# Grid attention of a two-model kernel: values held stationary, gates computed turned, the spatial norm on ScalarE and GpSimd

## The chip, the cores and the metric

The kernel runs on one core of one Trainium2 chip. The metric is the time of one execution in device microseconds, as the median of several runs. The core has five engines that run their own instruction streams in order and wait for one another by semaphores: TensorE (matrix products, PE in the profile, with weight loads as PEld), VectorE (DVE), ScalarE (ACT), GpSimd (POOL) and SyncE (SP), which here issues the large DMA transfers. TensorE writes to eight banks of PSUM of 128x512 fp32 values; a bank can be written again when an engine has read it and said so.

## The reference

Two blocks are computed one after the other, in fp32. The first has two layers of a mixture of retention, sparse attention and gated linear attention. The second has two layers on 256 tokens and 256 context tokens, D = 1024. The change lies in the second block's first layer, for 512 rows in all (4 tiles of 128; tiles 0 and 1 are tokens, 2 and 3 context):

```python
q, k, v, u, vv, gate = split(hl @ w_in)        # q 512, k 128, v 128, u 512, vv 512, gate 1024
a = windowed_sink_gqa(q, k, v, kc, vc, sink)   # 8 heads of 64, 2 key/value heads, softmax with a sink
b = chunk_gmlp(gelu(u), gelu(vv), ln_g, ln_b, w_s, b_s)
y = (concatenate([a, b], axis=-1) * silu(gate)) @ w_out
yc = (concatenate([ac, bc], axis=-1) * silu(gate_c)) @ w_out   # the same for the context rows

def chunk_gmlp(u, v, ln_g, ln_b, w_s, b_s):    # per chunk of 128 rows and group of 64 columns
    vn = layer_norm(v, ln_g, ln_b).reshape(B, n, 128, 8, 64)
    s = einsum('gpq,bnqgc->bnpgc', w_s, vn) + b_s
    return u * s
```

The softmax of one head divides by the sum of exp(logit - max) over the keys plus exp(sink - max). Token rows see 512 keys, context rows 256. In the second block's other layer (the odd layer) the attention is of another kind; it is not changed.

## The kernel before, in words

Products of high precision are made of three: each operand is split into a part rounded to fp32r ("high") and the rest ("low"), and TensorE adds high by high, high by low and low by high. Weight chunks come by DMA into a ring of three slots (`ring`); ScalarE copies a piece to the high part (`wide_high`), VectorE subtracts to get the low part (`wide_low`). For weights of the grid layer a chunk is four pieces of 128x1024, and the four chunks are e_g0 and e_g1 (the gate's two halves) and e_o0 and e_o1 (the output projection). The rows are `xhi` and `xlo`, turned so that the contraction lies on the partitions. `project_wide` (L1138) makes 24 products of 128x512 for one tile of rows.

The attention of the grid layer is a hand-written pipeline of `E_STEPS` = 15 steps, written once for each engine. There are 24 units (`E_UNITS`): a token tile with one head, or a context tile with two heads, so a unit always has 512 logits per row. In step g, TensorE does in this order:

1. a gate projection if `E_GATES` has one (e_g0 for tiles 0 to 3 in steps 0 to 3, e_g1 in steps 7 to 10);
2. row sums of a modulation chunk (`E_SUMS`, L734), their columns (`E_ADA`, L742), gate rows (`E_ROWS_AT`, L1157);
3. the turning of the probabilities of pair g-2 (`e_turn`, units 2g-4 and 2g-3, L771);
4. the logits of pair g (`e_logits_pair`, L1235, 64 contraction rows, the two units side by side in the row halves);
5. the value products of pair g-3 (`e_values`, L1219), with turned probabilities stationary and values moving, into bank `eo{t}` as rows by heads;
6. in step 4 the spatial products of `w_s` with the normed `evv` (`gs0` to `gs3`, L1290); in steps 12 and 13 the turning of gated rows (`turn_mixed`, eight blocks of 128x128 for a tile); in step 14 the first output projection.

ScalarE applies tanh to a gate (L1803), copies turned probabilities out of the bank (L1449), takes the exponentials with their row sums (L1819, L1824), and once for a tile the sink's exponential (L1836). VectorE finishes the gate's silu (`e_silu`, L2618), scales and masks the logits (L2650), reduces the maximum (L2653), takes the minimum with the negated sink (L2655), adds the sink (L2663), does two operations of the spatial norm in each of steps 0 to 3 (L2590, L2592), adds and multiplies the spatial results (L2679), and makes the low pieces (L2559). The division by the softmax's sum comes last, in `e_gated` (L2601 to L2610), on the 128x512 result of a tile, followed by the product with the gate. `e_mixed` (L2626) makes the spatial half of the gated rows. ScalarE and VectorE then split the turned rows into `xhi` and `xlo` (L1755, L2634).

Banks 0 and 1 are given in turn to projections, sums, columns, gate rows and spatial products (`proj()`); banks 4 and 5 hold the logits of a pair, 6 and 7 turned probabilities, 2 and 3 the attention results. The order in which the banks' users appear in `units_of_layer_e` is the order in which they must be freed. GpSimd rotates queries and keys before the stage and is idle in it. Chunks are loaded in the order of the list `CHE`, each when the last user of its slot is done.

## Time and profile before

| | us |
|---|---|
| median of 3 runs (1067.85 to 1070.85) | 1068.13 |
| the profiled execution, its own time | 1068.55 |
| its span, first to last instruction | 1066.2 |
| TensorE busy | 1034.2 (97%) |
| VectorE busy | 611.4 (57%) |
| ScalarE busy | 487.0 (46%) |
| GpSimd busy | 76.4 (7%) |
| mean granted TensorE clock | 0.995 |

A busy share is an average over the whole span. Products are pipelined: the duration shown for one product overlaps the next, so the price of a block of products is the distance between its start and the start of what follows it. A product of two fp32 operands is recorded as two instructions, so sixteen instructions are eight products.

### The profile page before, as it was taken

What the parts mean: (1) busy time and instruction counts of PE and PEld (TensorE: products, weight loads), DVE (VectorE), ACT (ScalarE), POOL (GpSimd) and SP (SyncE); (2) the same over time, 40 slices, a digit from 0 to 9 for tenths busy, and PEclk for the clock granted to TensorE, in tenths of its full rate; (3) what the DMA queues carried; (4) which work ended last, traced back from release to release, by engine and by line L of the source; (5) the groups of instructions that cost most, each with busy time, mean ns of one, the idle gap of its engine ahead of it and who ended that gap; (6) DMA issues with size and microseconds to landing.
All of it is one profiled execution on the core that took longest, in us unless ns stands there. A gap on an engine that the chain in (4) does not pass through costs nothing.

```text
span 1066.2 us, 13509 instructions
## 1 busy us (share of the span) xinstructions
PE 1034.2 (97%) x5180; PEld 759.1 (71%) x5180; DVE 611.4 (57%) x1193; ACT 487.0 (46%) x958; POOL 76.4 (7%) x103
## 2 busy tenths in 40 slices
PE   7999999999999999999999999999999999999997
PEld 5788875777466887767875587777767888646565
DVE  2539866595656299754454653234754546135873
ACT  2536546562135365475540453246444433334872
POOL 3001110000000020110000000500000001212000
PEclk9999999999999999999999999999999999999999
DMA  9854442476625355235567353422443014433000
GB/s 384 314 200 166 158 158 81 158 312 270 251 88 197 135 195 202 106 115 216 218 237 310 124 199 121 158 99 80 182 178 137 4 40 157 179 111 146 2 1 39
DMA packets 13742, 171.27 MB, mean 161 GB/s; under 512 B 1504, under 2 KB 1760, under 8 KB 3056
## 3 DMA queue, kind: packets, MB, share of 16 engines
q1 hardware_dynamic: 13216, 168.82, 41.4%
q10 hardware_dynamic: 464, 1.61, 0.4%
q8 instruction: 41, 0.67, 0.3%
q14 instruction: 21, 0.17, 0.0%
HBM read 169.37 MB, written 1.05 MB: 160 GB/s over the span
## 4 chain that ended last, share of the span: by engine, by line
PE 83%; ACT 7%; DVE 6%; DMA 2%; issue 1%; SPq 0%; DVEq 0%; ACTq 0%
PE bank L800 15%; PE bank L1138 8%; PE bank L1087 8%; PE bank L1027 7%; PE bank L1185 6%; PE bank L771 5%; PE bank L1120 4%; PE bank L778 3%; PE bank L1322 3%; PE bank L872 3%; PE bank L1417 2%; PE bank L1144 2%; PE bank L1402 2%; PE bank L734 2%; DMA X<-in_x 1%; PE bank L1387 1%
## 5 line engine op out<-in xcount | busy, mean ns | idle before, releaser
L1526 ACT ACTIVATE whi<-ring 128x512 fp32r<-128x512 f32 x120 | 73.8, 629 | 67.8 <-PE bank L800 67.6
L800 PE MATMUL bank<-whi,xhi 128*128 128x512 f32 (+1 forms) x256 | 99.4, 388 | 1.3 <-ACT dsag L1449 1.3
L2208 DVE TENSOR_TENSOR wlo<-ring,whi 128x512 fp32r<-128x512 f32 x120 | 82.3, 707 | 29.8 <-ACT whi L1526 29.6
L800 PE MATMUL bank<-whi,xlo 128*128 128x512 f32 (+1 forms) x256 | 98.0, 383 | 0.0
L800 PE MATMUL bank<-wlo,xhi 128*128 128x512 f32 (+1 forms) x256 | 97.5, 381 | 0.0
L778 PE MATMUL bank<-ring,hT 128*128 128x512 f32 (+1 forms) x160 | 61.8, 540 | 1.8 <-ACT hT L1469 1.8
L1027 PE MATMUL bank<-merge_high,xhi 128*128 128x512 f32 x144 | 58.7, 408 | 1.6 <-ACT retqkv L1449 1.1
L800 PEld LDWEIGHTS bank<-whi,xhi 128*128 128x128 f32 x256 | 48.2, 188 | 12.6 <-ACT dsag L1449 1.6
L1027 PE MATMUL bank<-merge_high,xlo 128*128 128x512 f32 x144 | 57.0, 396 | 0.0
L1027 PE MATMUL bank<-ring_low,xhi 128*128 128x512 f32 x144 | 56.7, 394 | 0.0
L800 PEld LDWEIGHTS bank<-wlo,xhi 128*128 128x128 f32 x256 | 48.2, 188 | 9.9
L800 PEld LDWEIGHTS bank<-whi,xlo 128*128 128x128 f32 x256 | 48.1, 188 | 9.9
L2397 DVE TENSOR_TENSOR ring_low<-ring,merge_high 128x1024 fp32r<-128x1024 f32 x36 | 42.5, 1222 | 18.8 <-ACT merge_high L1626 18.6
L1138 PE MATMUL bank<-ring_low,xhi 128*128 128x512 f32 x128 | 50.5, 394 | 0.0
L778 PEld LDWEIGHTS bank<-ring,hT 128*128 128x128 f32 x160 | 29.8, 190 | 28.6 <-issue 20.1
L1684 ACT ACTIVATE out_high<-ring 128x1024 fp32r<-128x1024 f32 x16 | 15.6, 1045 | 65.8 <-DMA ring<-in_weights 65.8
L2109 DVE SCALAR_TENSOR_TENSOR retqkv<-ring,cst,retqkv 128x512 f32<-128x512 f32 x56 | 42.1, 752 | 2.0
L1626 ACT ACTIVATE merge_high<-ring 128x1024 fp32r<-128x1024 f32 x36 | 36.0, 1053 | 9.7 <-PE bank L1027 9.7
L1138 PE MATMUL bank<-wide,xhi 128*128 128x512 f32 x96 | 39.0, 406 | 0.2 <-DVE ring_low L2559 0.2
L1185 PE MATMUL bank<-whi,xhi 128*128 128x512 f32 x96 | 38.4, 400 | 0.0
L2554 DVE TENSOR_TENSOR ring_low<-ring,whi 128x1024 fp32r<-128x1024 f32 x12 | 15.6, 1302 | 39.1 <-ACT whi L1737 39.1
L1185 PE MATMUL bank<-ring_low,xhi 128*128 128x512 f32 x96 | 38.0, 395 | 0.0
(432 smaller groups left out, 2267.3 us busy)
## 6 DMA issues: line engine op xcount, KB each, us to landing
ring<-in_weights SPq DMA_DIRECT2D x73, 2048.0 KB, 8.1
ring<-in_weights SPq DMA_DIRECT2D x5, 1024.0 KB, 5.1
ring<-in_weights SPq DMA_DIRECT2D x2, 1360.0 KB, 9.7
ring<-in_weights SPq DMA_DIRECT2D x1, 1536.0 KB, 10.1
kk<-in_k SPq DMA_DIRECT2D x1, 1120.0 KB, 8.3
X<-in_x SPq DMA_DIRECT2D x1, 1024.0 KB, 15.2
kc<-in_k ACTq DMA_DIRECT2D x1, 1024.0 KB, 12.0
X<-in_context SPq DMA_DIRECT2D x1, 1024.0 KB, 10.2
```

Of the source, the lines that this page charges most:

```text
L771: mm = pe.transpose(ps[0:n, i * P:(i + 1) * P], blk, ident[:])
L778: mm = pe.matmul(ps[:, 0:width], hT[:, k, t * P:(t + 1) * P], ring[:, slot, k * width:(k + 1) * width], start=(k == 0), stop=(k == KD - 1))
L800: mm = pe.matmul(o[:, 0:width], a, b[:, q % BUFFERS, at], start=(k == 0 and m == 0), stop=(k == KD - 1 and m == 2))
L1027: mm = pe.matmul(o[:, :], a, b, start=(k == 0 and n == 0), stop=(k == KD - 1 and n == 2))
L1087: mm = pe.matmul(ps[:, :], branchT[b][:, k, t * P:(t + 1) * P], ring[:, slot, k * D + h * 512:k * D + h * 512 + 512], start=(k == 0), stop ...
L1120: mm = pe.matmul(ps[:, :], a, b, start=(k == 0 and m == 0), stop=(k == KD - 1 and m == 2))
L1138: mm = pe.matmul(ps[:, :], a, b, start=(k == 0 and n == 0), stop=(k == KD - 1 and n == 2))
L1185: mm = pe.matmul(o[:, :], a, b, start=(k == 0 and m == 0), stop=(k == KD - 1 and m == 2))
L1526: act.activation(whi1[:, q % BUFFERS, :], w, ACT.Copy).then_inc(event("hi1_ready"), 1)
L2109: ins = dve.scalar_tensor_tensor(rows, w, cst[:, k, v:v + 1], rows, ALU.mult, ALU.add)
L2208: dve.tensor_tensor(wlo1[:, q % BUFFERS, :], piece1(q)[2], whi1[:, q % BUFFERS, :], ALU.subtract).then_inc(event("lo1_ready"), 1)
L2397: dve.tensor_tensor(rest, w, whole, ALU.subtract).then_inc(event("merge_low"), 1)
```

## The change

- **Values stationary.** `e_values` takes a pair of units. The values (64 columns) are stationary, the turned probabilities (128 columns) move, and the result comes out turned: head dimension on partitions, rows along the bank. The even head writes to partitions 0 to 63, the odd head to 64 to 127.
- **Division earlier.** A result with heads on the partitions can't be divided by a sum per row, so the probabilities are divided before they are turned: `e_normal(g)` runs at the head of VectorE's step g+1, and the sink's argument and exponential are made for each pair, not for each tile.
- **Gates turned.** The first gate chunk is computed with weights stationary and rows moving (`gates_e`), into `egT`. `e_gated` is then one operation. The attention half of the gated rows needs no turning: ScalarE copies it to `xhi` (`attended_high`), VectorE subtracts (`attended_low`). `turn_mixed` turns four blocks for a tile and not eight.
- **Spatial norm.** ScalarE multiplies by the reciprocal deviation before step 0, GpSimd multiplies by the gain and adds the offset.
- **Other steps.** The second gate chunk is projected in steps 5, 6, 8 and 9 (before 7 to 10), the spatial products in steps 2 and 3 (before 4), with the weight pieces in steps that fit. The first two high pieces of e_g1 go to the buffer `whi`, so that they needn't wait for the last user of `wide`.

```diff
-E_GATES = {0: 0, 1: 1, 2: 2, 3: 3, 7: 4, 8: 5, 9: 6, 10: 7}
+E_GATES = {0: 0, 1: 1, 2: 2, 3: 3, 5: 4, 6: 5, 8: 6, 9: 7}
+E_SPATIAL = {2: (0, 1), 3: (2, 3)}
+E_HIGHS = {2: ((1, 0),), 3: ((1, 1), (1, 2), (1, 3)), 10: ((2, 0), (2, 1)), 11: ((2, 2), (2, 3))}
+E_LOWS = {2: ((1, 0),), 3: ((1, 1),), 4: ((1, 2),), 11: ((2, 0),), 12: ((2, 1), (2, 2)), 13: ((2, 3),)}
...
+        def step_heads(g):
+            t, heads = E_UNITS[2 * g]
+            return t, slice(heads[0], E_UNITS[2 * g + 1][1][-1] + 1)
...
+            if E_WIDE[j] == "e_g1" and i < 2:
+                return ring[:, slot, c], whi[:, i, :], ring_low[:, slot, c]
...
+            def gates_e(j):
+                ps = begin(le, f"e_g0{j}")
+                for k in range(KD):
+                    if k % 2 == 0:
+                        pe.wait_ge(event("wide_low"), k // 2 + 1)
+                    at = k * 512 + j * P
+                    whole, rest = wide[:, k, j * P:(j + 1) * P], ring_low[:, SLOT2["e_g0"], at:at + P]
+                    for n, (a, b) in enumerate(((whole, xhi), (rest, xhi), (whole, xlo))):
+                        mm = pe.matmul(ps[:, :], a, b[:, k, :], start=(k == 0 and n == 0), stop=(k == KD - 1 and n == 2))
+                done(le, f"e_g0{j}", mm)
...
             def e_turn(i):
-                if E_UNITS[i][0] < TT:
-                    pe.wait_ge(event("e_exp"), i + 1)
-                else:
-                    emptied(pe, u, f"el{i}")
+                pe.wait_ge(event("e_norm"), i + 1)
...
-                for a, h in enumerate(heads):
+                for a in range(len(E_UNITS[units[0]][1])):
                     for b in range(nb):
-                        mm = pe.matmul(o[:, h * 64:(h + 1) * 64], PT2e[:, i % 4, (a * nb + b) * P:(a * nb + b + 1) * P],
-                                       ev[:, b0 + b, (h // 4) * 64:(h // 4) * 64 + 64], start=(b == 0), stop=(b == nb - 1))
+                        for r, i in enumerate(units):
+                            h = E_UNITS[i][1][a]
+                            mm = pe.matmul(o[64 * r:64 * r + 64, (h // 2) * P:(h // 2 + 1) * P],
+                                           ev[:, b0 + b, (h // 4) * 64:(h // 4) * 64 + 64],
+                                           PT2e[:, i % 4, (a * nb + b) * P:(a * nb + b + 1) * P],
+                                           start=(b == 0), stop=(b == nb - 1))
...
             def turn_mixed(t):
-                for h in range(2):
-                    ps = begin(u, f"eyT{t}{h}")
-                    done(u, f"eyT{t}{h}", turn_blocks(ps, [eg[:, t, (4 * h + i) * P:(4 * h + i + 1) * P] for i in range(4)]))
+                ps = begin(u, f"eyT{t}")
+                done(u, f"eyT{t}", turn_blocks(ps, [eb[:, t, i * P:(i + 1) * P] for i in range(4)]))
...
-                if g == 4:
+                if g in E_SPATIAL:
                     slot = landed2("e_ws")
                     pe.wait_ge(event("ln_ready"), NT)
-                    for j in range(4):
+                    for j in E_SPATIAL[g]:
...
+            def attended_high(t):
+                emptied(act, u, f"eo{t}")
+                c = slice(t * P, (t + 1) * P)
+                act.activation(xhi[:, 0:4, c], egT[:, :, c], ACT.Copy).then_inc(event("ea_high"), 1)
...
             act.activation(st2[:, 24:28], st2[:, 20:24], ACT.Sqrt).then_inc(event("ln_std"), 1)
+            act.wait_ge(event("ln_root"), 1)
+            for t in range(NT):
+                act.activation(evv[:, t, :], evv[:, t, :], ACT.Copy, scale=st2[:, 54 + t:55 + t]).then_inc(event("ln_scaled"), 1)
...
+                    act.wait_ge(event("e_arg"), g + 1)
+                    t, heads = step_heads(g)
+                    act.activation(es2[:, t, heads], es2[:, t, heads], ACT.Exp).then_inc(event("e_es"), 1)
+                for j, n in E_HIGHS.get(g, ()):
                     wide_high(j, n)
                 if g in E_TURNED:
                     mixed_high(E_TURNED[g])
+                if g in (9, 11, 14):
+                    attended_high({9: 0, 11: 1, 14: 2}[g])
...
+            for t in range(NT):
+                pool.wait_ge(event("ln_scaled"), t + 1)
+                step(pool.tensor_tensor(evv[:, t, :], evv[:, t, :], lng, ALU.mult))
+                settle()
+                pool.tensor_tensor(evv[:, t, :], evv[:, t, :], lnb, ALU.add).then_inc(event("ln_ready"), 1)
...
+            def e_normal(g):
+                t, heads = step_heads(g)
+                dve.wait_ge(event("e_es"), g + 1)
+                if t < TT:
+                    dve.wait_ge(event("e_exp"), 2 * g + 2)
+                else:
+                    emptied(dve, u, f"el{2 * g}")
+                    emptied(dve, u, f"el{2 * g + 1}")
+                step(dve.tensor_tensor(r2[:, t, heads], sm2[:, t, heads], es2[:, t, heads], ALU.add))
                 settle()
+                step(dve.reciprocal(r2[:, t, heads], r2[:, t, heads]))
+                settle()
+                for i in (2 * g, 2 * g + 1):
+                    n = 512 // len(E_UNITS[i][1])
+                    for a, h in enumerate(E_UNITS[i][1]):
+                        v = L2e[:, i % 4, a * n:(a + 1) * n]
+                        ins = dve.tensor_scalar(v, v, r2[:, t, h:h + 1], None, ALU.mult)
...
+                    ins.then_inc(event("e_norm"), 1)
             def e_gated(t):
...
-                dve.tensor_tensor(etmp.rearrange("p (h d) -> p h d", h=8), ps[:, :].rearrange("p (h d) -> p h d", h=8),
-                                  r2[:, t, 0:8].unsqueeze(2).broadcast_to([P, 8, 64]), ALU.mult).then_inc(free(u, f"eo{t}"), 1)
...
+                v = egT[:, :, t * P:(t + 1) * P]
+                dve.scalar_tensor_tensor(v, ps[:, :].rearrange("p (j c) -> p j c", j=4), 0.5, v, ALU.mult,
+                                         ALU.mult).then_inc(free(u, f"eo{t}"), 1)
+            def attended_low(t):
+                dve.wait_ge(event("ea_high"), t + 1)
+                c = slice(t * P, (t + 1) * P)
+                dve.tensor_tensor(xlo[:, 0:4, c], egT[:, :, c], xhi[:, 0:4, c], ALU.subtract).then_inc(event("ea_low"), 1)
...
             for g in range(E_STEPS):
+                if g in E_ADA and g not in E_GATES:
+                    mod_out(u, E_ADA[g], int(E_ADA[g][-1]), e_which(E_ADA[g]), (1, 2))
+                if 1 <= g < 13:
+                    e_normal(g - 1)
+                if g == 5:
+                    wide_low(1, 3)
                 if g in E_GATES:
                     e_silu(E_GATES[g] // 4, E_GATES[g] % 4)
...
-                if g < NT:
-                    spatial_norm(g)
...
+                if g in (10, 12, 14):
+                    attended_low({10: 0, 12: 1, 14: 2}[g])
```

## Rows read from the trace of the kernel before

**Rows 1.** the chain that ended last, shares of the span (profile page, part 4)

```profile
PE 83%; ACT 7%; DVE 6%; DMA 2%; issue 1%; SPq 0%; DVEq 0%; ACTq 0%
```

**Rows 2.** busy us and instructions of each engine in one stretch, clock, DMA

```profile
753.24:775.68 22.44, 21.20 (x145) 15.21 (x145) 17.55 (x35) 12.80 (x26) 0.00 (x0) 1.00 0.69 268
```

**Rows 3.** TensorE's waits, 715 to 895: us in total, times, longest

```profile
PE bank L1290 <- DVE eu L2679: 1.0, 1, 1.0
PE bank L1157 <- DVE mod L2096: 0.7, 1, 0.7
```

**Rows 4.** the chain in order of time: start, us, what

```profile
754.40 0.70 DVE hT L2650
```

**Rows 5.** TensorE in order of time, steps 3 and 4: start, us, what

```profile
746.61 0.50 PE L1138 MATMUL bank<-wide,xhi 128*128 128x512 f32 x1
...
752.28 1.03 PE L771 MATMUL bank<-ident,hT 128*128 128x128 f32 x8
753.24 1.13 PE L1235 MATMUL bank<-ekT,eqT 64*128 64x512 f32 x4
754.30 2.00 PE L1219 MATMUL bank<-ev,hT 128*128 128x64 f32 x16
756.14 1.04 PE L771 MATMUL bank<-ident,hT 128*128 128x128 f32 x8
```

**Rows 6.** TensorE in order of time, the first block's gated scores

```profile
128.77 1.06 PE L955 MATMUL bank<-Y,KL 64*128 64x128 f32 x16
129.76 0.50 PE L800 MATMUL bank<-whi,xhi 128*128 128x512 f32 x1
```

**Rows 7.** TensorE by line and form: count, busy us, mean ns of one

```profile
L771 PE MATMUL bank<-ident,eg 128*128 128x128 f32 x32 | 4.2, 273 | 0.0
```

**Rows 8.** VectorE in order of time, grid attention

```profile
733.69 0.69 DVE L2618 SCALAR_TENSOR_TENSOR eg<-eg,bank 128x512 f32<-128x512 f32 x1 [1.78 <-ACT eg L1803]
734.29 0.69 DVE L2650 SCALAR_TENSOR_TENSOR hT<-bank,kk 128x512 f32<-128x512 f32 x1
...
737.33 0.74 DVE L2590 SCALAR_TENSOR_TENSOR evv<-evv,st,kk 128x512 f32<-128x512 f32 x1
...
757.56 0.17 DVE L2663 TENSOR_TENSOR es<-mx,col 128x8 f32<-128x8 f32 x1
...
762.07 1.65 DVE L2679 SCALAR_TENSOR_TENSOR eu<-bank,col,eu 128x256 f32<-128x256 f32 x4
...
811.15 2.35 DVE L2530 TENSOR_TENSOR Y<-ident,mod 128x1024 f32<-128x1024 f32 x2
```

**Rows 9.** VectorE by line and form, 722 to 895

```profile
L2559 DVE TENSOR_TENSOR ring_low<-ring,wide 128x1024 fp32r<-128x1024 f32 x8 | 9.3, 1219 | 0.0
```

**Rows 10.** VectorE in order of time: today's division, and the odd layer's normalisation

```profile
800.64 0.16 DVE L2601 TENSOR_TENSOR r<-sm,es 128x8 f32<-128x8 f32 x1
...
801.07 0.69 DVE L2606 TENSOR_TENSOR evv<-bank,r 128x512 f32<-128x512 f32 x1
...
986.36 0.88 DVE L2777 TENSOR_SCALAR LP<-LP,r 128x512 f32<-128x512 f32 x2
```

**Rows 11.** ScalarE in order of time, grid attention

```profile
733.00 0.60 ACT L1803 ACTIVATE eg<-bank 128x512 f32<-128x512 f32 x1
...
757.56 0.72 ACT L1819 ACTIVATE hT<-hT,mx 128x512 f32<-128x512 f32 x1 [0.70 <-DVE mx L2655]
...
764.80 0.19 ACT L1836 ACTIVATE es<-es 128x8 f32<-128x8 f32 x1
...
822.83 2.01 ACT L1749 ACTIVATE wide<-ring 128x1024 fp32r<-128x1024 f32 x2
```

**Rows 12.** GpSimd at 118, VectorE beside it, and that line's mean

```profile
118.39 1.29 POOL L2009 TENSOR_TENSOR KL<-gkT,Y 128x512 f32<-128x512 f32 x1 [34.61 <-ACT Y L1580]
...
118.80 1.43 DVE L2208 TENSOR_TENSOR wlo<-ring,whi 128x512 fp32r<-128x512 f32 x1 [1.22 <-ACT whi L1526]
...
L2208 DVE TENSOR_TENSOR wlo<-ring,whi 128x512 fp32r<-128x512 f32 x120 | 82.3, 707 | 29.8 <-ACT whi L1526 29.6
```

More of the change, by code:

```diff
@@ L251, in units_of_layer_e @@
                     u.append((f"eo{t}", 2 + t % 2))
-        if g == 4:
-            u += [(f"gs{j}", proj()) for j in range(4)]
+        u += [(f"gs{j}", proj()) for j in E_SPATIAL.get(g, ())]
         if g in E_TURNED:
-            u += [(f"eyT{E_TURNED[g]}{h}", (4, 0)[E_TURNED[g]] + h) for h in range(2)]
-    u += [(f"eyT{t}{h}", (4, 0)[t % 2] + h) for t in range(2, NT) for h in range(2)]
+            u.append((f"eyT{E_TURNED[g]}", (5, 1)[E_TURNED[g]]))
+    u += [(f"eyT{t}", (5, 1)[t % 2]) for t in range(2, NT)]
     u += [(f"eout{t}0", (6, 7, 2, 3)[t]) for t in range(NT)]
@@ L543, in e_rows @@
         def e_rows(name):
-            return eg[:, int(name[-1]), 0:512] if name in E_EARLY.values() else msum2[E_ROWS.index(name) % 2]
+            return egT[:, int(name[-1]), :] if name in E_EARLY.values() else msum2[E_ROWS.index(name) % 2]
+        def step_heads(g):
+            t, heads = E_UNITS[2 * g]
+            return t, slice(heads[0], E_UNITS[2 * g + 1][1][-1] + 1)
         def e_which(name):
@@ L1134, in project_wide @@
                     hi, low = xhi[:, k, t * P:(t + 1) * P], xlo[:, k, t * P:(t + 1) * P]
-                    whole = wide_late if j == len(E_WIDE) - 1 else wide
-                    rest = ring_low[:, SLOT2[E_WIDE[j]], k * 512:(k + 1) * 512]
-                    for n, (a, b) in enumerate(((hi, whole[:, k, :]), (hi, rest), (low, whole[:, k, :]))):
+                    at = slice((k % 2) * 512, (k % 2) * 512 + 512)
+                    _, whole, rest = wide_piece(j, k // 2)
+                    for n, (a, b) in enumerate(((hi, whole[:, at]), (hi, rest[:, at]), (low, whole[:, at]))):
                         mm = pe.matmul(ps[:, :], a, b, start=(k == 0 and n == 0), stop=(k == KD - 1 and n == 2))
                 done(u, name, mm)
+            def gates_e(j):
[8 more added lines that the diff above has]
+                done(le, f"e_g0{j}", mm)
             def project2(u, name, slot, t, width):
@@ L1745, in wide_high @@
                         act.wait_ge(event("eb_ready"), NT)
-                    elif j > 0:
-                        filled(act, u, f"e_g{j - 1}{NT - 1}")
+                    elif E_WIDE[j] == "e_o0":
+                        filled(act, u, f"e_g1{NT - 1}")
+                if E_WIDE[j] == "e_g1" and i == 2:
+                    filled(act, u, f"e_g0{NT - 1}")
                 w, whole, _ = wide_piece(j, i)
@@ L1832, in _ @@
                     mixed_high(E_TURNED[g])
-                for t in range(NT):
-                    if g == E_LAST[t] // 2 + 1:
-                        act.wait_ge(event("e_arg"), t + 1)
-                        act.activation(es2[:, t, :], es2[:, t, :], ACT.Exp).then_inc(event("e_es"), 1)
+                if g in (9, 11, 14):
+                    attended_high({9: 0, 11: 1, 14: 2}[g])
+            attended_high(3)
             mixed_high(2)
@@ L2659, in _ @@
                             dve.scalar_tensor_tensor(m, m, 0.125, ns, ALU.mult, ALU.min).then_inc(event("e_max"), 1)
-                for t in range(NT):
-                    if g == E_LAST[t] // 2:
-                        dve.wait_ge(event("e_max"), E_LAST[t] + 1)
-                        dve.tensor_tensor(es2[:, t, :], mx2[:, t, 0:8], sink, ALU.add).then_inc(event("e_arg"), 1)
-                if g < NT:
-                    spatial_norm(g)
+                    dve.wait_ge(event("e_max"), 2 * g + 2)
+                    t, heads = step_heads(g)
+                    dve.tensor_tensor(es2[:, t, heads], mx2[:, t, heads], sink[:, heads], ALU.add).then_inc(event("e_arg"), 1)
                 if g in E_GATES and E_GATES[g] >= 4:
@@ L2672, in _ @@
                         diagonal(DG2[v], v)
-                if g == 4:
-                    for j in range(4):
+                if g in E_SPATIAL:
+                    for j in E_SPATIAL[g]:
                         ps = filled(dve, u, f"gs{j}")
```

86 lines of the change are left out of this document (37 added, 49 removed).

## The prediction

> **What bounds the kernel now.** I read the chain of waits first. TensorE has 83% of it [rows 1], so time is gained by taking work from TensorE, unless a wait comes in its place. The second view is the busy time by stretch. The change lies in the fifteen steps of the grid attention, from 725 us to the end of the output products near 888. In the thinnest stretch there TensorE still works 21.20 of 22.44 us, VectorE 17.55 [rows 2]. Third, TensorE's own waits in this stage: 1.0 us for the spatial products, 0.7 for a bank that VectorE frees [rows 3], and 0.4 in two small ones; 2.1 us in all. Fourth, the chain inside that stretch: between 754 and 765 it goes through VectorE, operation after operation [rows 4]. That is the warning. Where a step has no wide projection, VectorE is already level with TensorE, and the change gives VectorE and ScalarE more to do in each step.
>
> **Prices of one step on TensorE** [rows 5]. A gate projection 5.67 us (746.61 to 752.28), turning a pair of units 0.96, logits of a pair 1.06, values of a pair 1.84.
>
> **Value products.** Today 16 instructions with stationary probabilities (128 columns to load) and 64 moving columns take 1.84 us. Afterwards the values are stationary (64 columns), 128 columns move, and two units stand side by side in the two column halves. No row has this form. The nearest is the gated score product: 16 instructions of 128 moving columns, in pairs over the two row halves, from 128.77 to 129.76, 0.99 us [rows 6]. If the pairs did not overlap at all, a block would stay at 1.84 or so; the lower end is what the score product leaves without start and end, about 0.86. I take 0.99: 12 blocks by 0.85 are 10.2 us less.
>
> **Turned gates.** The first gate chunk comes out turned, with as many products of the same width, so it costs the same. Half of the 32 turns of the gated rows go [rows 7]; at 0.96/8 = 0.12 us each, that is 1.9 us less. With the 2.1 us of waits, which lose their place, TensorE could win 14.2 us.
>
> **Prices on VectorE.** Gate product 0.60 us (733.69 to 734.29); the logits of a pair 3.04 (734.29 to 737.33); the sink argument 0.17; four spatial operations, that is two banks, 1.65 [rows 8]. A low piece of a weight chunk is 1.22 alone, about 1.15 in a row [rows 9]. The new normalisation: sum and reciprocal 0.43 (800.64 to 801.07), then two scalings, whose form exists in the odd layer, 0.80 to 0.88 for both [rows 10]; 1.23 us for each pair, now at the head of the next step. It needs the sink's exponential, and that follows the pair's last exponential (0.72 and 0.19 us) [rows 11]. From the last maximum to the start of the normalisation I count 1.06 us, in which VectorE, which runs in order, does nothing. The gate product and the next logits are queued behind this wait. A light step thus takes 3.04 + 1.06 + 1.23 = 5.3 us on VectorE where TensorE needs 0.96 + 1.06 + 0.99 = 3.0.
>
> **The spatial norm.** Eight VectorE operations (1.4 us in each of steps 0 to 3) go. In their place ScalarE scales four rows before step 0. Two 128x1024 copies take 2.01 us, so 0.50 for 512 elements, 2.0 for four; the exponential's 0.72 would be the upper end, 2.9. With the wait for the reciprocal it is 2.3 us ahead of the first tanh, now at 733.00 [rows 11]; the first gate product moves from 733.69 to 736.0. GpSimd then does eight operations of 128x512 at 1.29 [rows 12], 10.9 us with gaps, from 732.6 to about 743.5. TensorE asks for the result near 748, in step 2, so that alone costs nothing (4 us of slack).
>
> **The steps in order**, without GpSimd's interference. Step 0: logits on VectorE until 739.7, normalisation 740.7 to 741.9. Step 1: TensorE comes for the logits banks at 737.9, and the second is read at 738.9: 1.0 us of waiting. VectorE: gate 742.5, logits 745.6, normalisation 746.6 to 747.9. Step 2: gate 748.5, logits 751.5, argument 751.7, and only then the first spatial bank, 752.5. TensorE has issued both spatial products of this step by 749.5, and its next projection uses that bank: 3.1 us of waiting. Step 3 has 5.67 us of projection, in which VectorE catches up; its logits start 1.1 after TensorE's (753.24 to 754.40 today [rows 4, 5]), at 760.3, and with two spatial banks and one low piece they last until 766.5. Step 4 is light: normalisation 767.7, logits and argument 770.9, low piece 772.1. Step 5: normalisation 773.3, last low piece 774.5. TensorE reaches the second gate chunk at 766.1; it waits for the third piece, 2.9, and for the last, 0.9: 3.8 us. From there to step 9 projections of 5.7 us cover VectorE, and nothing is lost. DMA: the chunks on the ring are asked for by events that move with TensorE; the closest, the small spatial weights, are issued 20 us before step 2. Nothing there.
>
> Step 9 has the diagonals of 2.35 us [rows 8] and then the pair's normalisation, logits, gating and the new low part in step 10, before VectorE frees the bank that the gate rows need: 1.9 us instead of 0.7 today. In steps 11 to 13 ScalarE has exponentials, four copies of weights (two are 2.01 [rows 11]), gate rows, turned pairs and the new high part. The last turn then waits for its bank: 1.6 us.
>
> **The sum:** new waits 1.0 + 3.1 + 3.8 + 1.9 + 1.6 = 11.4 us, against 14.2: 2.8 us less.
>
> **What GpSimd does to VectorE.** At 118.39 a GpSimd operation of 1.29 us runs. A VectorE subtraction of two SBUF tensors starts at 118.80 and takes 1.43 us [rows 12], where 0.71 is the mean of its line; it ends 0.54 after GpSimd's end. So it was held. Between 732.6 and 743.5 GpSimd is always busy, and VectorE's two minima and its sink argument of step 0 read two SBUF tensors, though tiny ones, on which no row of before tells. If each waits for the operation under way, the normalisation of step 0 starts 3.1 us later, and the chain up to step 3 has no slack for it. Lower end 0. I take 2.0: they are small, but of the kind that was held. Remaining gain: 0.8 us.
>
> The Trainium skill ("SBUF — State Buffer", section "SBUF: two separate sides") says the two engines share a port pair under an exclusive lock, taken also by a VectorE operation with two SBUF inputs against a GpSimd operation that reads SBUF. By that rule size does not matter and the full 3.1 applies, which would make the change cost 0.3 us. The row at 118.80 agrees with the lock; none before shows a tiny operation.
>
> The profiled run took 1068.55 us (span 1066.2), 0.4 above the median. 1068.55 - 0.8 = 1067.7, against the median some 1067.3.
>
> **Rivals.**
> 1. *The vector chain is shorter* (25%). The tiny operations are not held, and value blocks take 0.86. 0.8 + 2.0 + 10 blocks by 0.13 = 4.1 us gained, and a little of the late waits too: 1064.0, down to 1062. For it: TensorE's saving is certain in kind. Against it: the waits are read from an in-order chain with little play.
> 2. *The column halves do not overlap* (8%). Place: the twelve value blocks, which stay at 1.84. 10.2 us are lost, less the two blocks covered in steps 3 and 4 and the two before the late wait (1.7 + 1.6): 6.9 us, 1074.2. From 1.1 us per block on the change no longer gains; the row halves of the score product speak against it.
> 3. *Every hand-over costs more* (15%). Place: the return trip from VectorE to ScalarE and back in steps 0 to 5, if 1.06 us is really 1.9, because ScalarE is in a copy when the maximum comes. Five trips by 0.8 are 4.0: 1071.3, slower. It decides from 0.2 us a trip on. For it: ScalarE has turned pairs and weight pieces in the same queue. Against: in steps 0 and 1 that queue is empty.
> 4. *GpSimd or the norm is late for the spatial products* (2%): 4 us of slack, so included in the range.
>
> **How the numbers follow.** The forecast has 50%, with its own range of 1065 to 1070. No change is what a measurement of this kernel can't tell from zero, 0.3% or 3.2 us: 1064.9 to 1071.3. Faster: rival 1 and a tenth of the forecast, 0.30. Slower: rival 2 and half of rival 3, 0.16. The rest, 0.54, is no change. The range goes from 1062.5 into rival 3, 1071.8; what is left out is rival 2 and the tail of rival 1.
>
> **What would show it.** Value blocks near 1.0 us; TensorE waiting for VectorE's spatial banks at the head of step 3, for a low piece in step 5, and for the logits bank in step 1; VectorE's minima and argument of step 0 as long as 0.5 to 1.3 us (held) or 0.16 (free); idle VectorE of about 1 us ahead of each normalisation; the last turn waiting for ScalarE. I am wrong if steps 1 to 5 hold less than 5 us or more than 13 us of waiting, or if the blocks stay above 1.2.

## The result, and the profile after

| | before | after |
|---|---|---|
| median, same chip | 1068.77 us (6 runs) | 1075.66 us (6 runs, 1073.45 to 1079.33) |
| profiled execution | 1068.55 us, span 1066.2 | 1073.65 us, span 1071.4 |
| ratio of the times | | 1.0059, 95% interval 1.0037 to 1.0082 |
| unaltered again, another chip | 1070.18 us (29 runs) | 1074.76 us (12 runs); ratio 1.0046, 1.0030 to 1.0061 |

The change is slower by 4.6 to 6.9 us by the medians, 0.46% to 0.59% by the ratios (the ratio is that of all executions of one chip and not exactly the quotient of the medians). The forecast was 1067.3 us, range 1062.5 to 1071.8, and its likeliest case was no change. It was wrong in sign and in size.

The chain of the profile page of the kernel after, part 4 (in place of [rows 1]): TensorE's share fell from 83% to 80%, ScalarE's and VectorE's rose.

```profile
PE 80%; ACT 9%; DVE 7%; DMA 2%; issue 2%; SPq 0%; DVEq 0%; ACTq 0%
```

TensorE's waits in the grid attention, after (in place of [rows 3]): total, times, longest, us.

```profile
PE bank L1147 <- DVE ring_low L2602: 3.0, 1, 3.0
PE bank L1159 <- DVE eu L2736: 2.9, 1, 2.9
PE bank L1260 <- DVE hT L2710: 2.1, 1, 2.1
PE bank L1178 <- DVE mod L2139: 1.6, 1, 1.6
PE bank L780 <- ACT hT L1474: 1.6, 1, 1.6
PE bank L1315 <- DVE egT L2673: 1.0, 1, 1.0
```

The five forecast waits are there: the low piece in step 5, the spatial bank at the head of step 3, the logits bank of step 1, the gate rows, the last turn. A sixth was not forecast: 1.0 us in step 2, where the spatial products wait for the bank of a gate (L1315). They sum to 12.2 us against 2.1 before.

TensorE in order of time, after, steps 3 and 4 (in place of [rows 5, 6]): start, us, what; in brackets the wait.

```profile
752.74 1.13 PE L1315 MATMUL bank<-evv,ring 128*128 128x256 f32 x4 [0.97 <-DVE egT L2673]
756.75 0.50 PE L1159 MATMUL bank<-xhi,wide 128*128 128x512 f32 x1 [2.88 <-DVE eu L2736]
757.09 0.39 PE L1159 MATMUL bank<-xhi,ring_low 128*128 128x512 f32 x1
...
758.31 0.63 PE L1159 MATMUL bank<-xlo,wide 128*128 128x512 f32 x1
...
763.98 1.03 PE L780 MATMUL bank<-ident,hT 128*128 128x128 f32 x8
764.95 1.13 PE L1260 MATMUL bank<-ekT,eqT 64*128 64x512 f32 x4
766.00 1.09 PE L1242 MATMUL bank<-hT,ev 128*64 128x128 f32 x16
768.86 1.04 PE L780 MATMUL bank<-ident,hT 128*128 128x128 f32 x8
```

Two things are to be seen. The value block is short, as forecast: 1.09 us with its tail, and the next group starts 1.02 to 1.03 after it in all twelve. And the gate projection, whose products are the same in number and size as before, lasts from 756.75 to 763.98, 7.23 us instead of 5.67: one product takes 0.39 us at 757.09 and 0.63 at 758.31. The windows of the same kernel say why. Columns: stretch and its length, busy us and instructions of TensorE, its weight loads, VectorE, ScalarE and GpSimd, granted clock, DMA share, GB/s.

```profile
752.00:757.00 5.00, 1.38 (x5) 0.93 (x6) 4.83 (x12) 2.30 (x7) 0.00 (x0) 1.00 0.02 3
757.00:761.00 4.00, 4.00 (x12) 3.09 (x12) 2.83 (x7) 0.61 (x1) 0.00 (x0) 0.58 0.00 0
774.00:778.00 4.00, 0.96 (x6) 0.45 (x4) 3.82 (x9) 1.72 (x5) 0.00 (x0) 1.00 0.53 213
778.00:782.00 4.00, 4.00 (x11) 3.09 (x12) 2.18 (x4) 0.00 (x0) 0.00 (x0) 0.57 0.02 8
```

In the first and third window TensorE mostly waits (1.38 of 5.00 us busy, 0.96 of 4.00). Right behind each, the granted clock is 0.58 and 0.57: it stands at its lower level, 1.2 GHz, for one stretch of 3.4 us each (from 757.6 and from 778.1), and TensorE does half the work in it. That is 1.7 us lost per stretch, 3.4 in all, and the forecast has no such term.

ScalarE and VectorE in order of time, after, step 0 (in place of [rows 8, 10, 11]), and GpSimd beside them (in place of [rows 12]).

```profile
733.80 2.56 ACT L1833 ACTIVATE evv<-evv,st 128x512 f32<-128x512 f32 x4 [0.25 <-DVE st L2629]
```

```profile
738.30 0.69 DVE L2673 SCALAR_TENSOR_TENSOR egT<-egT,bank 128x512 f32<-128x512 f32 x1 [4.54 <-ACT egT L1838]
...
740.35 0.79 DVE L2715 TENSOR_TENSOR mx<-mx,nsink 128x1 f32<-128x1 f32 x1
...
742.49 1.22 DVE L2715 TENSOR_TENSOR mx<-mx,nsink 128x1 f32<-128x1 f32 x1
743.75 0.17 DVE L2722 TENSOR_TENSOR es<-mx,col 128x2 f32<-128x2 f32 x1
744.69 0.40 DVE L2640 TENSOR_TENSOR r<-sm,es 128x2 f32<-128x2 f32 x1 [0.78 <-ACT es L1866]
...
746.12 0.68 DVE L2673 SCALAR_TENSOR_TENSOR egT<-egT,bank 128x512 f32<-128x512 f32 x1
...
748.16 0.16 DVE L2715 TENSOR_TENSOR mx<-mx,nsink 128x1 f32<-128x1 f32 x1
```

```profile
741.19 1.27 POOL L2081 TENSOR_TENSOR evv<-evv,kk 128x512 f32<-128x512 f32 x1
742.42 1.28 POOL L2079 TENSOR_TENSOR evv<-evv,kk 128x512 f32<-128x512 f32 x1
743.78 1.29 POOL L2081 TENSOR_TENSOR evv<-evv,kk 128x512 f32<-128x512 f32 x1
```

The minimum of one column takes 0.16 us at 748.16, when GpSimd is done (743.78 + 1.29), and 1.22 at 742.49, where it ends with GpSimd's operation (742.42 + 1.28 = 743.70). Two minima and one sum are longer by 0.63 + 1.06 + 0.24 = 1.93 us.

**The stage as a sum.** The stage runs from the first turned keys to the odd layer's first product. The columns are its length, what TensorE waited in it (the length less its busy time), and the time at half clock in the clock record of each trace; the next is TensorE's busy time less half of that, which is its work at full clock. The last two put the stage's length of the profiled execution, and the ratio of the times of all executions (as us of 1070), against before.

| kernel | stage | waiting | half clock | work | stage - before | ratio as us |
|---|---|---|---|---|---|---|
| before | 165.2 | 2.2 | 0 | 163.1 | | |
| after | 168.2 | 12.2 | 6.8 | 152.7 | +3.0 | +6.3 |
| after, again | 168.1 | 12.1 | 6.8 | 152.5 | +2.8 | +4.9 |

So 10.4 us of work and 2.2 of old waits went, 12.2 of waits and 3.4 of slow clock came: +3.0. The rest of the profiled difference of 5.1 us lies mostly ahead of the stage (1.85 us): a half-clock stretch from 337.8, in code that is the same in both. It begins in a group of products that stands behind the same wait of 1.5 us in both kernels, before and then after:

```profile
337.36 4.81 PE L778 MATMUL bank<-ring,hT 128*128 128x340 f32 x16 [1.51 <-ACT hT L1469]
337.32 6.50 PE L787 MATMUL bank<-ring,hT 128*128 128x340 f32 x16 [1.50 <-ACT hT L1494]
```

In 13 profiles of changed kernels such a stretch stands between 335 and 343 in nine.

The mean granted clock, which is recorded for every execution, says how much there is of this outside the profiled ones. It is 0.988 on average over the 12 executions of the changed kernel run again, against 0.994 over the 29 of before, and 0.994 when the waits are filled (the second filled run below, where before has 0.994 too). The profiled executions of the changed kernel have 0.991 and 0.992. As an estimate, 0.006 of 1070 us are some 6.4 us lost to the clock; that is an upper bound, since a slow clock costs nothing while TensorE waits.

### The profile page after: what moved, and what is told of

Read it like the earlier page. It is cut to its first block, busy times and chain, and to the rows that moved or that the text cites. A ratio compares the mean times of both kernels' runs of the same rounds, so it can differ in the third digit from the quotient of the medians.

```text
span 1071.4 us, 13547 instructions
## 1 busy us (share of the span) xinstructions
PE 1028.8 (96%) x5164; PEld 747.9 (70%) x5164; DVE 619.8 (58%) x1237; ACT 490.2 (46%) x970; POOL 86.6 (8%) x111
## 4 chain that ended last, share of the span: by engine, by line
PE 80%; ACT 9%; DVE 7%; DMA 2%; issue 2%; SPq 0%; DVEq 0%; ACTq 0%
PE bank L809 15%; PE bank L1096 8%; PE bank L1036 7%; PE bank L1206 6%; PE bank L1147 6%; PE bank L780 5%; PE bank L1129 4%; PE bank L787 3%; PE bank L1347 3%; PE bank L881 3%; PE bank L1442 2%; PE bank L1165 2%; PE bank L1427 2%; PE bank L743 2%; PE bank L751 1%
## 5 line engine op out<-in xcount | busy, mean ns | idle before, releaser
L1036 PE MATMUL bank<-ring_low,xhi 128*128 128x512 f32 x144 | 56.6, 393 | 0.0
L1147 PE MATMUL bank<-ring_low,xhi 128*128 128x512 f32 x96 | 38.7, 403 | 0.0
L1206 PE MATMUL bank<-whi,xlo 128*128 128x512 f32 x96 | 37.9, 395 | 0.0
L1206 PE MATMUL bank<-ring_low,xhi 128*128 128x512 f32 x96 | 37.8, 393 | 0.0
## 6 DMA issues: line engine op xcount, KB each, us to landing
X<-in_context SPq DMA_DIRECT2D x1, 1024.0 KB, 10.4
```

What stands on the lines that cost most here:

```text
L1036: mm = pe.matmul(o[:, :], a, b, start=(k == 0 and n == 0), stop=(k == KD - 1 and n == 2))
L1147: mm = pe.matmul(ps[:, :], a, b, start=(k == 0 and n == 0), stop=(k == KD - 1 and n == 2))
L1206: mm = pe.matmul(o[:, :], a, b, start=(k == 0 and m == 0), stop=(k == KD - 1 and m == 2))
```

## The experiments

Theories: **clock** (the new waits cost more than their length, since the clock falls behind them), **bank** (the bank order makes the wait of step 3), **GpSimd** (it holds VectorE), **queue** (ScalarE's order stretches the hand-over). Each run was timed against the kernel before on its own chip; there were three chips, so runs of different chips are compared by their ratios to before.

**The change again.** No edit.

> The changed kernel once more, unaltered, as the measure for the others on the same chip. Theory A (waits plus clock): TensorE stands idle for about 2 to 3 us at the logits of step 1, at the head of step 3 and in step 5, and after one or two of these waits the granted clock is at half, 1.2 GHz, for 3.4 us, which costs 1.7 us each; so 1073 to 1079 us, and runs of one kernel differ by multiples of 1.7 us. Theory B (the additional time has nothing to do with the clock but with slower products in the turned form): the same time in every run, and blocks of 24 turned products above 5.7 us everywhere.

Ratio 1.0046 (1.0030 to 1.0061). The waits are the same to 0.1 us, and the stretches are again at the same places in the stage.

**Filled waits.** TensorE multiplies ones into a bank that is free, in the two long waits; nothing reads it.

```diff
+FILL3, FILL5 = 10, 11
...
+                    if k == 4 and name == "e_g10":
+                        keep_busy(bank[3], FILL5)
...
+                if g == 3:
+                    keep_busy(bank[3], FILL3)
```

> Ten products of ones (128x128) into a bank that is not in use at the head of step 3, and eleven between the fourth and fifth row block of the first e_g1 projection: they do no work, they only keep TensorE busy in the two waits of 2.9 and 3.0 us. Theory A (the half clock follows from the waits): the waits stay, the granted clock keeps 1.00 in steps 3 and 5, and the time falls by 1.7 to 3.4 us against the changed kernel. Theory B (products in the turned form are slow, or the clock falls by chance): no difference beyond 1 us, or slower by the added products.

Ratio 1.0021 (1.0004 to 1.0037), on the chip of the run before it: 1072.27 us against 1074.76, 12 executions each. TensorE, filled waits, then the windows:

```profile
754.57 2.39 PE L775 MATMUL bank<-ones 128*128 128x128 f32 x20
757.29 0.50 PE L1162 MATMUL bank<-xhi,wide 128*128 128x512 f32 x1 [0.32 <-DVE eu L2741]
773.75 2.62 PE L775 MATMUL bank<-ones 128*128 128x128 f32 x22
```

```profile
757.00:761.00 4.00, 3.71 (x16) 3.06 (x17) 3.36 (x8) 1.14 (x4) 0.00 (x0) 1.00 0.00 0
778.00:782.00 4.00, 3.33 (x21) 1.63 (x23) 1.62 (x3) 0.60 (x1) 0.00 (x0) 1.00 0.00 0
```

VectorE hands over no sooner, and 5 us of useless products were added, yet the stage is 2.1 us shorter and the clock is 1.00 where it was 0.58 and 0.57. Two stretches went, and one came, behind the 2.1 us wait of step 1; net that is the 1.7 us of one stretch, and the rest is waiting. The clock term is shown.

**Filled waits, step 1 too** (seven products more ahead of the logits of step 1).

```diff
+                if g == 1:
+                    keep_busy(bank[3], 7)
```

> As fill, and seven more products of ones ahead of the logits of step 1, where TensorE waited 2.1 us; with fill the one half-clock stretch left in the stage began right behind that wait. They do no work. Theory A: no half clock between 725 and 890 us in the trace; 1.0 to 1.7 us less than fill, so about the time of before plus 0 to 1.5 us. Theory B (chance): the same time as fill, with a half clock somewhere in the stage.

Ratio 1.0012 (1.0000 to 1.0024). No stretch is left in the stage, as Theory A says, but its length stays (166.0 both times), and the ratio is not clear of that of the run before. In steps 1 and 2 TensorE is ahead of VectorE, so time won there becomes waiting: 1.0 us in step 2 and 0.7 at the head of step 3, where the first filled kernel has 0 and 0.3.

**Normalisation between the units.** The normalisation of a pair moves behind the logits of the next pair's first unit.

```diff
-                if 1 <= g < 13:
+                if g == 12:
                     e_normal(g - 1)
...
+                        if i % 2 and g >= 1:
+                            e_normal(g - 1)
```

> The normalisation of the last pair is moved from the head of VectorE's step to between the two units of the step's logits, so that VectorE works on logits while ScalarE makes the exponentials. Theory A (the in-order hand-over of 1.06 us in each step is what makes VectorE late): no idle time of 0.78 us before the sum, the waits of steps 1, 3 and 5 shrink from 2.1, 2.9 and 3.0 us to about 1, 1 and 0 to 1, no half clock in the stage; 4 to 8 us less than the changed kernel, 1066 to 1070. Rival C (ScalarE or the spatial products set the pace, not VectorE's order): less than 1.5 us of difference.

Ratio 1.0100 (1.0068 to 1.0132), much slower, and the expectation failed. VectorE's idle time moved from the normalisation (0.78 us) to the wait for the tanh, 1.26 us in steps 1 and 2: ScalarE runs in order, and the second exponential, now later, stands before it. The waits grew to 15.5 us, the half clock to 13.7.

**The turned forms alone.** Stationary values and turned gates stay; the spatial norm goes back to VectorE, the spatial products to step 4, the second gate chunk to steps 7 to 10.

```diff
-E_GATES = {0: 0, 1: 1, 2: 2, 3: 3, 5: 4, 6: 5, 8: 6, 9: 7}
-E_SPATIAL = {2: (0, 1), 3: (2, 3)}
+E_GATES = {0: 0, 1: 1, 2: 2, 3: 3, 7: 4, 8: 5, 9: 6, 10: 7}
+E_SPATIAL = {4: (0, 1, 2, 3)}
...
```

> Only the first part of the change: values stationary, normalised probabilities, turned gates and half of the turning; the spatial norm stays on VectorE in steps 0 to 3, the spatial products in step 4 and the second gate chunk in steps 7 to 10, with the weight pieces where they were. Theory A (VectorE is behind in light steps, wherever these are): steps 4 to 6 have three light steps in a row, VectorE needs 5.3 us and TensorE 3.0 in each, so the waits there grow to 6 to 9 us with at least one half clock, and the kernel is at 1070 to 1076, no better than the full change. Rival D (the spatial norm on ScalarE and GpSimd and the new steps are what costs time): 1060 to 1066, the gain on TensorE shows.

Ratio 1.0017 (1.0003 to 1.0032), as Theory A says; Rival D is refuted. The waits fall only from 12.2 to 9.7, and the half clock is 10.2 us. TensorE waits 3.3 us for a low piece and 3.2 for the spatial banks, now in other steps. So the moved steps alone did not bring the waits; most of them are there with the turned forms alone, which put their work on VectorE (103.6 us busy in the stage against 92.3 before).

**Other banks for the spatial products.** They use the attended tiles' banks, free until step 3, and in step 3 one of these, instead of the projections' banks.

```diff
-        u += [(f"gs{j}", proj()) for j in E_SPATIAL.get(g, ())]
+        u += [(f"gs{j}", {0: 3, 1: 2, 2: 3}[j] if j < 3 else proj()) for j in E_SPATIAL.get(g, ())]
```

> The first three spatial products get banks 3 and 2 (free at that time) and not banks 0 and 1, so the projection of step 3 does not wait for VectorE to read the spatial result; nothing else changes. Theory A: the waits of 1.0 us in step 2 and 2.9 us at the head of step 3 go, and the half clock behind them; VectorE loses its idle 4.7 us in step 3; TensorE then comes earlier to step 5 and waits longer there (about 4 us, with a half clock). Net 2 to 6 us less than the changed kernel. Rival E (VectorE's chain alone sets step 5, so a wait is only moved): less than 1 us.

Ratio 0.9983 (0.9969 to 0.9997), faster than before. The waits of 1.0 and 2.9 us are gone, that of step 5 is 3.4. The half clock did not shrink, against the expectation: one stretch of 6.8 us, from 775.7, stands at the wait of step 5, part of it while TensorE still waits. A renaming of three banks gives 4.4 us of the stage.

**ScalarE's scalings later.** The four scalings behind the first tanh instead of ahead of it.

```diff
-            act.wait_ge(event("ln_root"), 1)
-            for t in range(NT):
-                act.activation(evv[:, t, :], ...)
...
+                if g == 0:
+                    act.wait_ge(event("ln_root"), 1)
+                    for t in range(NT):
+                        act.activation(evv[:, t, :], ...)
```

> Only the four scalings are moved behind the first tanh. Theory A: VectorE's chain starts 2.5 us earlier; step 1's wait of 2.1 us goes to about 0, the other waits shrink only where their chain has no idle time: 2 to 4 us less than the changed kernel, with one half clock less. Rival F: GpSimd's operations, now beside steps 0 and 1, hold VectorE for 2 us or more; less than 1 us of gain.

Ratio 1.0046 (1.0030 to 1.0061), no gain. Counted from the stage's start VectorE's first gate product comes 2.8 us earlier, but its second 0.8 us later than in the changed kernel. TensorE's wait of step 1 is gone, as expected, but one of 2.15 us stands in step 2 instead, and the half clock is 17.1 us. VectorE, scalings later:

```profile
735.63 1.29 DVE L2716 TENSOR_TENSOR mx<-mx,nsink 128x1 f32<-128x1 f32 x1
...
738.28 1.24 DVE L2716 TENSOR_TENSOR mx<-mx,nsink 128x1 f32<-128x1 f32 x1
739.56 1.22 DVE L2723 TENSOR_TENSOR es<-mx,col 128x2 f32<-128x2 f32 x1
741.04 1.10 DVE L2641 TENSOR_TENSOR r<-sm,es 128x2 f32<-128x2 f32 x1 [0.27 <-ACT es L1867]
...
742.38 2.72 DVE L2649 TENSOR_SCALAR hT<-hT,r 128x512 f32<-128x512 f32 x2
```

Now every such operation beside GpSimd is held, the normalisation's scalings too (2.72 us for two instead of 0.88): 6.0 us together. Rival F holds.

**Both, later scalings and other banks.** The two edits above together; in the expectation `gsbank` is the run with the other banks alone.

> gsbank, and ScalarE's four scalings of the spatial rows (2.56 us) stand behind the first gate's tanh and not ahead of it. Theory A: VectorE starts step 0 about 2.5 us earlier, less 0 to 2 us for GpSimd, which now runs beside more of VectorE's operations with two SBUF inputs; the wait of step 1 goes below 1 us and the one of step 5 shrinks to 2 to 3 us. 1.5 to 3.5 us less than gsbank. Rival F (GpSimd holds VectorE as long as the scalings did): no difference to gsbank.

Ratio 0.9991 (0.9975 to 1.0007), against 0.9983 with the banks alone. Nothing is won by the later scalings; Theory A failed here too.

**No gain and bias.** GpSimd's eight operations are left out, and with them the spatial norm's gain and bias.

```diff
-                act.activation(evv[:, t, :], ..., scale=...).then_inc(event("ln_scaled"), 1)
+                act.activation(evv[:, t, :], ..., scale=...).then_inc(event("ln_ready"), 1)
...
-            for t in range(NT):
-                pool.wait_ge(event("ln_scaled"), t + 1)
-                step(pool.tensor_tensor(evv[:, t, :], evv[:, t, :], lng, ALU.mult))
-                settle()
-                pool.tensor_tensor(evv[:, t, :], evv[:, t, :], lnb, ALU.add).then_inc(event("ln_ready"), 1)
```

> The changed kernel with the multiplication by the gain and the addition of the bias of the spatial norm left out (the eight GpSimd operations beside step 0; ScalarE's scalings stay). This prices the GpSimd term alone. Theory: the operations held VectorE's minima and argument of step 0 for 2 to 3 us. Without them these take 0.16 us each, the first normalisation starts 2.3 to 3.1 us earlier, TensorE's 2.1 us wait for the logits bank in step 1 falls below 0.5, and the waits at the head of step 3 and in step 5 stay within 0.7 us of 2.9 and 3.0, each with its half-clock stretch behind it. So 1.5 to 3 us less than the changed kernel: ratio to before 1.0020 to 1.0035. Rival (the hold is absorbed, VectorE catches up in step 2 anyway): ratio 1.0045 or more.

Ratio 0.9998 (0.9981 to 1.0014), a larger gain than expected, although the wait of step 1 fell only to 1.5 us and not below 0.5. VectorE:

```profile
738.25 0.69 DVE L2667 SCALAR_TENSOR_TENSOR egT<-egT,bank 128x512 f32<-128x512 f32 x1 [4.54 <-ACT egT L1838]
...
741.81 0.16 DVE L2709 TENSOR_TENSOR mx<-mx,nsink 128x1 f32<-128x1 f32 x1
...
744.14 0.68 DVE L2667 SCALAR_TENSOR_TENSOR egT<-egT,bank 128x512 f32<-128x512 f32 x1
```

From one gate product to the next it takes 5.89 us instead of 7.82: GpSimd had cost 1.93, the very sum of the held rows above. The stage is 3.4 us shorter than that of the change run again: 1.6 of waiting and 1.7 of one half-clock stretch less. The 2.8 us wait at the head of step 3 is still there, but the clock keeps its upper level behind it. In the changed kernel a wait of 1.0 us (for the gate product that GpSimd delayed) stands 4 us ahead of the 2.9. So a delay of 1.9 us on VectorE cost 3.4 on TensorE in these profiles; that the small wait decided over the clock behind the 2.9 is not shown, since such stretches also come and go without it.

**Second gate chunk a step later**, on top of the other banks.

```diff
-E_GATES = {0: 0, 1: 1, 2: 2, 3: 3, 5: 4, 6: 5, 8: 6, 9: 7}
+E_GATES = {0: 0, 1: 1, 2: 2, 3: 3, 6: 4, 7: 5, 8: 6, 9: 7}
```

> Spatial banks taken from the attended tiles' banks (as in the run that was faster than before), and besides it the four products of the second gate chunk in steps 6 to 9 instead of 5, 6, 8 and 9. Theory: TensorE then does turning, logits and values of step 5 (3.0 us) while VectorE makes the last low pieces, so the 3.4 us wait in step 5 shrinks below 1 us and no half-clock stretch follows: 3 to 5 us less than the run with the banks alone, ratio to before 0.994 to 0.9955. Rival (VectorE's chain is the bound in steps 4 to 6 and the wait only turns into one for a logits bank): at most 1 us less, ratio 0.9975 or more.

Ratio 0.9936 (0.9914 to 0.9958). TensorE in order of time, this kernel:

```profile
768.53 1.09 PE L780 MATMUL bank<-ident,hT 128*128 128x128 f32 x8
770.14 1.13 PE L1260 MATMUL bank<-ekT,eqT 64*128 64x512 f32 x4 [0.52 <-DVE hT L2710]
771.20 1.09 PE L1242 MATMUL bank<-hT,ev 128*64 128x128 f32 x16
772.23 0.50 PE L1147 MATMUL bank<-whi,xhi 128*128 128x512 f32 x1
```

The turns, logits and values of step 5 stand where the 3.4 us wait was, 0.5 us of waiting is left, and no half-clock stretch follows. The one of 3.4 us that is left in the stage stands behind the 2.1 us wait of step 1.

**Late steps in another order**, on top of the other banks.

```diff
-... 11: ((2, 2), (2, 3))}
+... 11: ((2, 2),), 12: ((2, 3),)}
-                    attended_high({9: 0, 11: 1, 14: 2}[g])
+                    attended_high({9: 0, 12: 1, 14: 2}[g])
-                    e_gated({8: 0, 10: 1, 13: 2}[g])
+                    e_gated({8: 0, 11: 1, 13: 2}[g])
-                    attended_low({10: 0, 12: 1, 14: 2}[g])
+                    attended_low({11: 0, 13: 1, 14: 2}[g])
```

> The run with the spatial banks, and the late steps in another order: VectorE's gating of tile 1 and first low part in step 11 instead of 10, second low part in 13 instead of 12, ScalarE's last weight copy and second high part in step 12 instead of 11. Theory: the 1.6 us for the gate rows' bank falls to about 0.4, the 1.6 us of the last turn for ScalarE to about 0: 2.8 us less, ratio to before 0.9955 to 0.997. Rival (VectorE and ScalarE are full up to the output products, so the waits come back at project_mixed): ratio 0.998 or more.

Ratio 0.9967 (0.9950 to 0.9984), within the expectation. The 1.6 for the gate rows is 0.4, the 1.6 of the last turn 0.8, and 0.3 came at the output products: 1.7 us less of waiting there.

**All three.** Other banks, second chunk later, late steps reordered: the edits of the three runs together.

> Both: the spatial banks, the second gate chunk in steps 6 to 9, the late steps reordered. If both theories hold and add, 6 to 8 us less than the banks alone: ratio to before 0.991 to 0.993. If one of the rivals holds, 0.994 to 0.997.

Ratio 0.9919 (0.9894 to 0.9943), within the expectation: 1062.81 us against 1070.75, the profiled execution 1062.35 us. This version beats both kernels. Its waits (3.2 us for a logits bank are 2.1 in step 1 and 1.1 in step 5), and its stage (724.60 to 882.02):

```profile
PE bank L1260 <- DVE hT L2710: 3.2, 2, 2.1
PE bank L780 <- ACT hT L1474: 0.8, 1, 0.8
PE bank L1165 <- ACT hT L1517: 0.7, 1, 0.7
PE bank L1178 <- DVE mod L2139: 0.4, 1, 0.4
PE bank L1147 <- ACT hT L1474: 0.3, 1, 0.3
...
```

```profile
724.60:882.02 157.42, 152.57 (x913) 113.08 (x912) 100.13 (x221) 78.44 (x179) 10.19 (x8) 1.00 0.28 105
```

All kernels by the same sum as above:

| kernel | stage | waiting | half clock | work | stage - before | ratio as us |
|---|---|---|---|---|---|---|
| filled waits | 166.0 | 6.8 | 3.4 | 157.5 | +0.8 | +2.2 |
| filled, step 1 too | 166.0 | 6.6 | 0 | 159.4 | +0.8 | +1.3 |
| normalisation between | 174.8 | 15.5 | 13.7 | 152.5 | +9.6 | +10.7 |
| turned forms alone | 167.0 | 9.7 | 10.2 | 152.2 | +1.8 | +1.8 |
| other banks | 163.6 | 8.7 | 6.8 | 151.5 | -1.6 | -1.8 |
| scalings later | 170.5 | 11.0 | 17.1 | 151.0 | +5.3 | +4.9 |
| scalings, banks | 164.4 | 8.4 | 6.8 | 152.6 | -0.8 | -1.0 |
| no gain and bias | 164.7 | 10.5 | 3.4 | 152.4 | -0.6 | -0.2 |
| banks, chunk later | 160.0 | 6.2 | 3.4 | 152.1 | -5.3 | -6.9 |
| banks, late order | 162.4 | 6.6 | 6.8 | 152.4 | -2.9 | -3.5 |
| all three | 157.4 | 4.9 | 0 | 152.6 | -7.8 | -8.7 |

The work of the changed kernel is 151.0 to 152.7 us throughout (the low values are those where part of a long half-clock stretch was itself idle; the filled ones have their products on top). Everything else is waiting and clock.

## Why the prediction was wrong

**The step that failed** is the sum: it priced each new wait at its own length. "New waits 1.0 + 3.1 + 3.8 + 1.9 + 1.6 = 11.4 us, against 14.2" has no term for what comes behind a wait. Two of these waits are each followed by 3.4 us at 1.2 GHz, which cost 1.7 us apiece. Filling the two waits removes these stretches and makes VectorE no earlier, and the time falls. Without the clock the stage would be 0.4 us shorter than before (12.2 - 12.6), close to the forecast 0.8 and by its own account no change.

| term | forecast | measured |
|---|---|---|
| value blocks | -10.2 | -9.3 (21.58 to 12.31 us over all twelve) |
| half of the turns | -1.9 | -1.4 (3.27 to 1.83 us) |
| all work together | -12.1 | -10.4 |
| old waits | -2.1 | -2.2 |
| step 1, logits bank, with GpSimd's part | +1.0 | +2.1 |
| step 2, spatial product, head of step 3 | +3.1 | +1.0 and +2.9 |
| step 5, low pieces | +3.8 | +3.0 |
| gate rows, last turn | +1.9, +1.6 | +1.6, +1.6 |
| GpSimd | +2.0 | in the lines above; 1.93 on VectorE |
| half clock behind waits | none | +3.4 |
| stage | -0.8 | +3.0 |

The error of 3.8 us is 3.4 of clock and 1.7 of work oversized, less 1.2 of waits oversized. The work terms were mis-sized in two places. The values' price before, 1.84, is that of the blocks in steps 3 and 4, and the mean of all twelve is 1.80. The other prices came from near forms: 16 instructions of 128 columns take 0.99 us in row halves, and 1.03 in column halves; and 0.12 us for each turn, taken from the distance of a turn group to the logits behind it, was 0.09.

- *The value products* were right in kind: 1.84 to 1.03 us. Rival 2 is refuted.
- *The chain of VectorE* was right: the waits stand where it said, and steps 1 to 5 hold 9.0 us of them, inside the 5 to 13 that it named. So by its own signs the prediction would have passed; none of them looked at the clock. From the end of VectorE's last operation on the maximum (the minimum with the sink's) to the normalisation it is 0.97 us (0.78 of it idle) where ScalarE's queue is empty, not 1.06. The four scalings took 2.56 us instead of 2.0, and the first gate product came 2.8 us later in the stage instead of 2.3; by the run with later scalings that was worth nothing.
- *GpSimd* was sized right (2.0 against 1.93), but by luck: it holds part of the small operations when VectorE starts at 738.3 (the sink argument falls between two operations of GpSimd, at 743.75, and is free), and all, for 6.0 us, when it starts earlier. The Trainium skill ("SBUF — State Buffer", section "SBUF: two separate sides") speaks of an exclusive lock for the whole instruction, with two SBUF inputs or in a two-port mode. The rows agree for two inputs: 1.22 to 1.29 us for a 128x1 operation of 0.16. The two one-input scalings of 0.88 took 2.72; whether they run in such a mode no row shows.
- *Rival 3* (every hand-over costs more) does not stand in the changed kernel, but its mechanism, ScalarE's order, is what the normalisation between the units ran into.
- *The remaining time.* Of the 4.9 to 6.3 us by the ratios, the stage explains 2.8 to 3.0. For nine of the eleven other kernels stage and ratio agree within 1.1 us, so the untouched code adds little there. The rest of 2 to 3 us is not seen in the two profiles, but the clocks recorded for all executions point at it: a mean of 0.988 where the profiled ones have 0.991 and 0.992. As an estimate, 0.003 to 0.004 of 1070 us are 3 to 4 us, two half-clock stretches more in a typical execution. Where these stand is not recorded, so this part stays argued.

That waiting costs TensorE its clock is also what the Trainium skill says ("TensorE: Matmul & The Clock Gate", section "HAM oscillation — how this bites in real kernels"): a wait is paid once as a wait and again in the slow products behind it. The traces of after agree, with 0.58 and 0.57 behind waits of 2.9 and 3.0 us. The trace of before could have shown it as well. It has three stretches, none of them in the stage. One, from 236.2, stands 2.3 us behind a wait of 1.35 us; one, from 10.7, stands behind a wait of 2.1 us, and a group of the same form takes 1.92 us at full clock. TensorE, before:

```profile
9.88 2.65 PE L734 MATMUL bank<-ring,cst 128*32 128x512 f32 x16 [2.10 <-issue]
...
27.31 1.92 PE L734 MATMUL bank<-ring,cst 128*32 128x512 f32 x16 [0.71 <-issue]
```

Other waits of 1.5 and 1.6 us have no stretch behind them there, so the trace gave the price, 1.7 us, but not the chance.

## What to carry to other kernels

When a change takes work from TensorE and puts waits in its place, price each wait twice: its length, and 1.7 us more for a stretch at half clock that may follow. Before giving up such a change, look at what stands behind the waiting product: here other banks gave 4.4 us of the stage, projections moved behind independent work 3.7, and a late reordering 1.3 (on top of both 2.5, of which 1.7 are the stretch of step 1, which the reordering doesn't touch). Together they turned a loss of 0.5% into a gain of 0.8%. Work on GpSimd is not free beside VectorE, not even when VectorE's operations are tiny; what a delay of the bound chain costs is to be read where it ends.

## What was not expected of the hardware

- Half-clock stretches are 3.4 us long or a multiple (6.8 and 10.2). At waits of 2.8 us and more one stood in all of these profiles with two exceptions: the 2.84 us wait with no gain and bias, and 3.46 us at the head of step 3 with the normalisation between the units. Behind the same 2.1 us wait of step 1 one followed in four kernels (filled, normalisation between, chunk later, late order), but not in the changed kernel, with the banks alone, or in all three; behind the 1.5 us wait at 337 one followed in nine profiles of 14. Waits of equal length thus do not have one price.
- With the scalings later, a stretch from 749.0 lasted 10.2 us, in which TensorE also worked. So one bad place can cost several times the 1.7 us.
- A filler can pay: 5 us of useless products made the kernel 2.5 us faster than the unfilled one.
